# Rows of two expert tables fetched together: one 8 KB fetch a token and slot in a ring of two, in place of two 4 KB fetches in a ring of four

## The reference, cut to what matters

```
ub = u_tab[eb]
vb = v_tab[eb]
a = jax.nn.gelu(jnp.einsum('td,ted->te', xb, ub, preferred_element_type=jnp.float32))
return jnp.einsum('te,ted->td', (gb * a).astype(vb.dtype), vb)
```

## Time and profile before

| what | us |
|---|---|
| time, median of 3 runs | 2168.68 (2165.64 to 2168.92) |
| span of the profiled execution, first to last instruction | 2161.6 |
| median less that span | 7.1 |
| PE busy in the span | 2121.7 (98%) |
| DVE, ACT, POOL busy | 1442.4, 858.3, 1038.6 |

### The profile page before, as it was taken

How to read it: one execution, slowest core, us unless ns; L and a number is a source line. 1 busy time by engine, 2 the same in 40 slices (tenths; PEclk the granted TensorE clock), 3 DMA queues, 4 the chain that set the end, 5 groups by cost and what they waited for, 6 DMA issues and landing times.

```text
span 2161.6 us, 29125 instructions
## 1 busy us (share of the span) xinstructions
PE 2121.7 (98%) x10648; PEld 1837.8 (85%) x10648; DVE 1442.4 (67%) x2713; ACT 858.3 (40%) x1306; POOL 1038.6 (48%) x573
## 2 busy tenths in 40 slices
PE   8989999999999999999999999999999999999999
PEld 7857888888877877899999999999998888888887
DVE  5973411110054995369998777787867999999987
ACT  4354522232264454253334444444433333333332
POOL 1203244443423333435566888888863444444342
PEclk9999999999999999999999999999999999999999
DMA  4202344444442222334347899998899999999996
GB/s 177 82 27 62 104 117 127 117 119 115 117 118 74 86 71 77 117 106 121 112 147 207 242 267 321 284 315 249 261 309 318 388 388 371 373 375 377 369 359 251
DMA packets 240489, 444.14 MB, mean 205 GB/s; under 512 B 102459, under 2 KB 152028, under 8 KB 240220
## 3 DMA queue, kind: packets, MB, share of 16 engines
q1 hardware_dynamic: 152060, 299.07, 41.8%
q0 software_dynamic: 55488, 134.83, 19.3%
q10 hardware_dynamic: 32800, 8.39, 1.8%
HBM read 397.71 MB, written 44.50 MB: 205 GB/s over the span
## 4 chain that ended last, share of the span: by engine, by line
PE 69%; POOL 13%; DVE 8%; issue 4%; DMA 3%; ACT 2%; SPq 0%; DVEq 0%; ACTq 0%; POOLq 0%
PE bank L469 22%; PE bank L473 22%; PE bank L472 22%; POOL gate_matrices L1151 9%; POOL y L1160 4%; DMA y<-in_peer_u_rows,gidx 3%; DVE m L1979 1%; PE bank L923 1%; DVE xn L1980 1%; DVE WL L2297 1%; PE bank L645 1%; DMA wraw<-in_peer_u 1%; ACT sc L1302 1%; DVE y L2308 0%; DVE hots L2329 0%
## 5 line engine op out<-in xcount | busy, mean ns | idle before, releaser
L1140 POOL TENSOR_TENSOR WL<-wraw,WH 128x1024 fp32r<-128x1024 f32 x171 | 435.9, 2552 | 723.5 <-ACT WH L1191 723.5
L1191 ACT ACTIVATE WH<-wraw 128x1024 fp32r<-128x1024 f32 x411 | 435.0, 1060 | 627.4 <-PE bank L469 393.6
L469 PE MATMUL bank<-XH,WH 128*128 128x384 f32 (+2 forms) x1864 | 668.8, 359 | 12.6 <-DVE WL L2297 7.8
L473 PE MATMUL bank<-XH,WL 128*128 128x384 f32 (+2 forms) x1864 | 657.8, 353 | 0.0
L472 PE MATMUL bank<-XL,WH 128*128 128x384 f32 (+2 forms) x1864 | 657.6, 353 | 0.0
L469 PEld LDWEIGHTS bank<-XH,WH 128*128 128x128 f32 x1864 | 351.4, 189 | 46.3 <-issue 12.9
L472 PEld LDWEIGHTS bank<-XL,WH 128*128 128x128 f32 x1864 | 351.6, 189 | 29.0 <-issue 0.7
L473 PEld LDWEIGHTS bank<-XH,WL 128*128 128x128 f32 x1864 | 351.1, 188 | 28.7
L2297 DVE TENSOR_TENSOR WL<-wraw,WH 128x1024 fp32r<-128x1024 f32 x240 | 293.0, 1222 | 57.6 <-ACT WH L1191 51.8
L469 PE MATMUL bank<-WH,GH 128*128 128x512 f32 x768 | 298.9, 389 | 1.6 <-issue 1.6
L473 PE MATMUL bank<-WH,GL 128*128 128x512 f32 x768 | 298.8, 389 | 0.0
(11 more groups left out here) (313 smaller groups left out, 2561.8 us busy)
## 6 DMA issues: line engine op xcount, KB each, us to landing
wraw<-in_peer_u SPq DMA_DIRECT2D x128, 512.0 KB
wraw<-in_peer_v SPq DMA_DIRECT2D x128, 512.0 KB
activations<-ac SPq DMA_DIRECT2D x122, 192.0 KB
ar<-activations SPq DMA_DIRECT2D x122, 192.0 KB
gr<-gate_matrices SPq DMA_DIRECT2D x124, 128.0 KB
wraw<-in_w_gate SPq DMA_DIRECT2D x22, 512.0 KB
wraw<-in_w_up SPq DMA_DIRECT2D x22, 512.0 KB
wraw<-in_w_down SPq DMA_DIRECT2D x22, 512.0 KB
```

Of the source, the lines that this page charges most:

```text
L469: mm = pe.matmul(out, wh, xh, start=first, stop=False)
L473: return pe.matmul(out, wl, xh, start=False, stop=last)
L1140: pool.tensor_tensor(WL[:, u % NW, 0:m], wraw[:, u % NR, 0:m], WH[:, u % NW, 0:m].bitcast(F32), ALU.subtract).then_inc(s("w_lo"), 1)
L1191: act.activation(WH[:, u % NW, 0:k * n], wraw[:, u % NR, 0:k * n], ACT.Copy).then_inc(s("w_hi"), 1)
```

## The change

The two tables are laid side by side in memory, so that one indirect DMA of 8 KB a token brings the rows of u and v of one slot. There are 128 such fetches of 1 MB, in a ring of two buffers of 8 KB a partition. Each slot is finished before its buffer is free: DVE makes the dot product, ACT applies Gelu and multiplies by the gate (two instructions on 128x1), and DVE adds the row of v one unit later. Steps 0 and 1 of the up stage have no slot, 53 slots are begun in the other 93 steps, and 75 in the down stage. The scatters stand 1, 3, 3, 3, 3, 3 to the slots, so that 128 are out after 48 slots.

```diff
-NGATHER = 4
-EARLY = 2
-SCATTERS = [0, 2, 1, 2, 1, 2, 2, 1, 2, 1, 2]
+NGATHER = 2
+SLOTS_UP = 53
+SCATTERS = [1, 3, 3, 3, 3, 3]
-UP_ROWS_1, UP_ROWS_2 = 112, HS
+def slots_until(step):
+    if step < 2:
+        return 0
+    if step <= ups:
+        return (step - 1) * SLOTS_UP // (ups - 1)
+    return SLOTS_UP + min((step - ups) * (HS - SLOTS_UP) // (NEXP - 4), HS - SLOTS_UP)
+def slots_of(step):
+    return range(slots_until(step), slots_until(step + 1))
...
+        u_row, v_row = ([gathered[:, n, at:at + D] for n in range(NGATHER)] for at in (0, D))
+        uv_rows = A["peer_uv_rows"]
...
-            for row in range(2 * HS):
-                if row >= NGATHER:
-                    pool.wait_ge(s("rows_used"), row - NGATHER + 1)
+            for k in range(HS):
+                if k >= NGATHER:
+                    pool.wait_ge(s("rows_used"), k - NGATHER + 1)
+                pool.indirect_dma_start(out=gathered[:, k % NGATHER, :], out_offset=None, in_=uv_rows[:, :],
+                                        in_offset=bass.IndirectOffsetOnAxis(ap=gidx[:, k:k + 1], axis=0)
+                                        ).then_inc(s(f"row_landed{k % NGATHER}"), 16)
+                for n in range(scattered_until(k), scattered_until(k + 1)):
+                    scatter(n)
...
+            def activate_slots(step):
+                for k in slots_of(step):
+                    if k == 0:
+                        act.wait_ge(s("gates_copied"), 1)
+                    act.wait_ge(s("dots"), k + 1)
+                    act.activation(gdot[:, k:k + 1], gdot[:, k:k + 1], ACT.Gelu_apprx_tanh).then_inc(s("dots_active"), 1)
+                    act.wait_ge(s("dots_active"), k + 1)
+                    act.activation(gdot[:, k:k + 1], gdot[:, k:k + 1], ACT.Copy, scale=ggate[:, k:k + 1]).then_inc(
+                        s("slots_active"), 1)
...
+            def dot_slot(k):
+                dve.wait_ge(s(f"row_landed{k % NGATHER}"), 16 * (k // NGATHER + 1))
+                if k == 0:
+                    dve.wait_ge(s("x_nat_made"), 1)
+                at = u_row[k % NGATHER]
+                dve.tensor_tensor_reduce(out=at, in0=at, in1=x_nat[:, :], scale=1.0, scalar=0.0, op0=ALU.mult, op1=ALU.add,
+                                         accum_out=gdot[:, k:k + 1]).then_inc(s("dots"), 1)
+            def add_slot(k):
+                dve.wait_ge(s("slots_active"), k + 1)
+                if k:
+                    dve.wait_ge(s("rows_used"), k)
+                dve.scalar_tensor_tensor(out=hN[:, NTD, :], in0=v_row[k % NGATHER], scalar=gdot[:, k:k + 1],
                                          in1=hN[:, NTD, :], op0=ALU.mult, op1=ALU.add).then_inc(s("rows_used"), 1)
+            def use_slots(step):
+                for k in slots_of(step - 1):
+                    add_slot(k)
+                for k in slots_of(step):
+                    dot_slot(k)
...
-                for row in range(EARLY):
-                    use_row(row)
-                    use_rows(x - FIRST_GATE_UP)
+                    use_slots(x - FIRST_GATE_UP)
...
-    laid["peer_u_rows"] = laid["peer_u_2"][0]
+    laid["peer_uv_rows"] = _np.concatenate([laid["peer_u_2"][0], laid["peer_v_2"][0]], 1)
```

More of the change, by code:

```diff
@@ L94, in fours_of, with scattered_until @@
     return range(FIRST_FOUR + b * fours // GATE_UPS, FIRST_FOUR + (b + 1) * fours // GATE_UPS)
-def rows_until(slot):
+def slots_until(step):
     ups = NEXP - FIRST_GATE_UP
-    after = min(slot, GATE_UPS) + max(min(slot, ups) - GATE_UPS, 0)
-    rest = 2 * HS - EARLY - ups
-    return EARLY + after + min(max(slot - ups, 0) * rest // (NEXP - 4), rest)
-def scattered_until(row):
-    heads, part = divmod(row, len(SCATTERS))
+    if step < 2:
[5 more added lines that the diff above has]
+    return range(slots_until(step), slots_until(step + 1))
+def scattered_until(slot):
+    heads, part = divmod(slot, len(SCATTERS))
     return min(heads * SEL + sum(SCATTERS[:part]), HS)
-def slot_after_row(row):
-    return next(n for n in range(3 * NEXP) if rows_until(n) > row)
 def t5_bucket(dist):
@@ L1156, in _ @@
             pool.wait_ge(s("index_made"), 1)
-            for row in range(2 * HS):
-                if row >= NGATHER:
-                    pool.wait_ge(s("rows_used"), row - NGATHER + 1)
-                pool.indirect_dma_start(out=gathered[:, row % NGATHER, :], out_offset=None,
-                                        in_=(u_rows if row < HS else v_rows)[:, :],
-                                        in_offset=bass.IndirectOffsetOnAxis(ap=gidx[:, row % HS:row % HS + 1], axis=0)
-                                        ).then_inc(s(f"row_landed{row % NGATHER}"), 16)
-                for k in range(scattered_until(row), scattered_until(row + 1)):
-                    scatter(k)
-                if scattered_until(row) == HS > scattered_until(row - 1):
+            for k in range(HS):
[6 more added lines that the diff above has]
+                    scatter(n)
+                if scattered_until(k + 1) == HS > scattered_until(k):
                     pool.wait_ge(s("scattered"), 16 * HS)
@@ L1623, in copy_gates @@
                     act.dma_start(gd.rearrange("i j t -> j i t")[:, :, tt * GTOK:(tt + 1) * GTOK], Gs[:, tt % 2, :, :]).then_inc(s(f"g_out{tt}"), 16)
-            def activate_rows(slot):
-                for n, (first, end) in enumerate(((0, UP_ROWS_1), (UP_ROWS_1, UP_ROWS_2))):
-                    if slot == slot_after_row(end - 1) + 2:
-                        act.wait_ge(s("rows_used"), end)
-                        act.activation(gdot[:, first:end], gdot[:, first:end], ACT.Gelu_apprx_tanh).then_inc(
-                            s("rows_active"), 1)
+            def activate_slots(step):
[7 more added lines that the diff above has]
+                        s("slots_active"), 1)
             def high_weighed(x):
@@ L1643, in down @@
                         high_weighed(x + 2)
[L1644 removed]
+                    activate_slots(NEXP - FIRST_GATE_UP + x)
             prepare()
@@ L2319, in use_rows @@
-            def use_rows(slot):
-                for row in range(rows_until(slot), rows_until(slot + 1)):
-                    use_row(row)
+                at = u_row[k % NGATHER]
[6 more added lines that the diff above has]
+                dve.scalar_tensor_tensor(out=hN[:, NTD, :], in0=v_row[k % NGATHER], scalar=gdot[:, k:k + 1],
+                                         in1=hN[:, NTD, :], op0=ALU.mult, op1=ALU.add).then_inc(s("rows_used"), 1)
```

26 lines of the change are left out of this document (3 added, 23 removed).

## The result

The changed kernel takes 2209.17 us (median of 4 runs, 2202.44 to 2210.11) against 2168.80 us of the kernel before (4 runs beside it, 2165.64 to 2172.99): ratio 1.0168, 95% interval 1.0148 to 1.0188. The forecast was 2164.0 us, range 2159 to 2192. It was wrong in sign and outside its range. The first rival happened, the ring of two.

What follows compares the result with a forecast made beforehand. PE, busy in 98% of the span, was taken as the bound, with only 8.6 us of idle to save. Span 2161.6 - 4.7 = 2156.9 us, plus 7.1 us around it, gave 2164.0 us; range 2159 to 2192.

Steps and rivals of the forecast that it cites:

- The first rival: Down stage: the ring of two sets the pace if a fetch takes over 8.9 us; 2195 us at 9.9 us; chance 0.27.
- The floor: Whole span: at most PE's 8.6 us of idle can be saved, so the span can't fall below 2153.0 us.
- POOL in the up stage: POOL was full, 435 of 446 us, and set the rows' pace; after the change 362 us, at most 428.
- the list of signs: What would show the forecast right, such as up-stage row waits under 40 us and POOL's idle there ended by adds.
- The start of the up stage: Before 1215 us: with no slot in steps 0 and 1, PE's 4.7 us of waits go; bounds 0 and 8.6.
- ACT: Both stages: two small instructions and semaphores, some 0.7 us a slot, cost nothing; DVE waits for ACT in the up stage.
- The ring: Down stage: a fetch takes 7.7 us where 8.9 are allowed, leaving 1.2 us of room a cycle; cost 0.
- The lag: Down stage: a late row only moves DVE inside its unit; it may lag 5.8 us before PE stands, by `WL`.
- The rival's price: Down stage, ring of two: at a 9.9 us fetch (8.5 + 1.4) the cycle is 14.5 us, giving 2195 us.
- Around the span: Outside the span: 7.1 us, as in the median before, added to the span of 2156.9 us.

Runs made afterwards that it cites:

- before_late_start: The kernel before, with no fetched row used before step 2 of the up stage and 163 rows instead of 159 in the down stage; 2152.63 us, ratio 0.9918.
- low_first: The changed kernel with `low` put before the add and the dot of a unit in the down stage; 2200.69 us, ratio 1.0139.
- half_fetch: The changed kernel with each fetch bringing only u's 4 KB a token, the add reading the same buffer; 2171.82 us, ratio 0.9996.
- gl_ahead: The changed kernel with `low_weighed` two units ahead and before the dot in the down stage, the add before it; 2190.65 us, ratio 1.0097.
- split_fetch: The changed kernel with two 4 KB fetches a slot in the same two buffers, u refetched after its dot, v after its add; 2185.65 us, ratio 1.0078.
- add_after_weigh: The changed kernel with the add of the last unit's slot moved between `weigh` and `low_weighed` in the down stage; 2169.05 us, ratio 0.9986.

## Why the prediction was wrong, step by step

**The floor** held: nothing but PE's idle time could be saved, and `before_late_start` came down to it (span 2151.0 against the 2153.0 worked out; 2.5 us of it lie outside the two stages). It left one thing out: a wait can also cost clock, 1.7 us in the kernel before.

**POOL in the up stage: right in size, wrong as a cause.** The fetch took 1.33 us there, as assumed, and POOL's idle was ended by adds (87.9 us), as the list of signs said. But "it is full", "the rows arrive at POOL's pace" did not explain DVE's waits of the earlier trace rows. POOL made as many scatters and nearly as many fetches in `before_late_start` and waited for DVE; what was missing was its lead.

**The start of the up stage: right.** No wait of PE stands before 1215 us, DVE's waits for rows fell to 23.8 us (under 40 was the mark), and the stage is 5.5 us shorter against the 4.7 taken. Part of the agreement is luck: the eight profiled kernels with this up stage and 8 KB fetches took 462.1 to 469.2 us in it, against one trace of before. `before_late_start` shows that the later first use alone is enough for the gain; fewer fetches aren't needed.

**ACT: right in size.** Its two instructions take 0.20 and 0.295 us, and in the down stage ACT was in time. In the up stage DVE waited 23.8 us for it, as foretold. In the kernel as changed I see no wait of PE that comes from it; in `low_first` ACT's waits for dots are part of what holds up `WH`.

**The ring: here it failed.** "At 7.7 us the ring has 1.2 us of room a cycle." The allowance, 13.5 us less 4.6, was right: dot to release measured 3.30 + 1.28 = 4.58 us. The fetch was not: 10.6 us instead of 7.7 where DVE waited for it, so a turn of 15.4 us where 13.5 were allowed. Two terms of that were mis-sized. POOL's own part was taken as unchanged at 1.31 us. It was 2.43 in the mean (1.45 in the down stage of before) and 3.0 in the fetches that DVE waited for: 1.7 of the 2.9 us. The second is the flight behind it, 7.6 us in these fetches against 7.7 - 1.31 = 6.4: the 6.27 us of the earlier trace rows came from the up stage, and its single row is not this stage's. The sum also left out the 0.28 us from the release to the fetch. I had the earlier trace rows with 2.68 us on POOL and 10.55 us to the dot, and set it aside because "these had other fetches of the same queue before them". "With starts 6.75 us apart there is rarely one" was wrong too: a fetch that takes over 6.75 us is never alone, and the prediction's own 7.7 us is over it. The two in the timeline run from 1980.99 to 1991.95 and from 1987.62 to 1998.63. The added 4 KB, the term that the change was about, was right: 1.3 us (`half_fetch`) against the 1.4 added.

The Trainium skill, page "DMA: Bandwidth & Descriptors", section "Anatomy of one DMA — SWDGE (gpsimd) path", gives by its fit an estimate of 2.0 + 2.4 = 4.4 us for such a fetch. The measurement differs (7.6 us behind the issue, with the DMA engines 93% busy), and decides.

**The lag: wrong in its place.** "DVE may lag 5.8 us before PE stands" went by `WL`, wanted two units after. `low_weighed` makes `GL` for the next unit and stands directly in front of the wait for the row, so a late row delays the next unit's `GL`, and PE stands after one unit's room. By the sum it matters little: with a turn 1.34 us too long any lag is used up after a few turns. No run shows that by itself, since `gl_ahead`, which has more lag, brought other waits in.

**The rival's price.** It was given 2195 us at a fetch of 9.9 us, against 2209 measured. Its 8.5 us before the added 1.4 came from no row. At 10.6 us in every turn it would have been 2195 + 37.5 x 0.7 = 2221; 22 of the 68 fetches were not waited for, so the mean turn was 14.84 us and not the 15.2 of that sum. The room of "a slower PE leaves the DMAs more room" was small (DMA share 0.93 against 0.97), and the fetch was not quick for it.

**Around the span: wrong.** 7.1 us was taken from a median and the span of one execution; it is 2.1 us. The profiled execution of before was a quick one (about 2163.7), and the forecast stood 5 us too high against its own sum. This decides nothing here.

**Open.** How much a short issue alone would give back, since `low_first` brought another wait in; why the issue is held up, and why not each time; how much of `split_fetch` is the earlier release; 5 us of the down stage; the 7 us of `before_late_start` that no span shows.

## What to carry to other kernels

Before a ring is made shorter, add up one whole turn (use, release, issue, flight, landing to next use) from rows of the busy stage where it will run, take the longest fetch seen there rather than a quiet one, and compare with the turn that the bounding engine allows: here 13.5 us were allowed and the mean turn was 14.8, which cost 52 us; a third buffer took back all but 3. Joining two fetches also joins their releases: the first half's buffer is given back only with the second's. And where a producer is hardly faster than its consumer, a consumer that starts too early may wait for it through the whole stage; try a later first use before cutting the producer's work.

## What the runs showed of the hardware

**A POOL fetch is longer to issue beside some of DVE's work.** In the changed kernel's down stage its instruction took 0.94 us while DVE was idle. Where it began beside `low` it took 2.68 us, if DVE went on through the two `ga` and `GL` and stopped, and mostly 3.82 with a dot and a further `low` behind them. In `low_first` it took 1.08 us beside the two `ga` and `GL`, though DVE was busy then too. It can be seen in before as well: 2.68 us. So how busy DVE is does not decide alone. What runs beside it doesn't either: in `add_after_weigh` the same sequence of DVE gave 1.01 us 28 times and over 3 us eight times. The Trainium skill, page "SBUF — State Buffer", section "Who interferes with whom", has DVE and GpSimd share one pair of SBUF ports under an exclusive lock, and has a DVE instruction with two SBUF inputs contend with a GpSimd instruction that reads SBUF. The longer issues agree with that (all of these DVE instructions have two inputs there); the short ones beside the same instructions it does not explain. The same section says that `tensor_tensor` did not stall a DMA of GpSimd in a probe, and infers the reason; the 2.68 and 3.82 us here against 0.94 speak against that for this indirect DMA. No run here took the two inputs away, so the cause is not shown.

**Short waits can cost PE more than their length.** Behind four of its waits in the down stage, the shortest of 1.82 us, the matmuls ran for 3.4 us at the lower clock level. The length of the wait does not tell alone: behind one of 3.36 us and one of 2.58 us the clock stayed up.

**A threshold.** With three or four buffers two slots take 13.4 to 13.5 us, which is PE's own pace, and the stage 526 to 529 us; the ring then has room for 20 or 27 us a turn. With two buffers, the turns of 13.66, 13.98 and 14.84 us went with 533.1, 540.3 and 574.7 us. The slope, some 36 us for each us of turn ((574.7 - 526) / 1.34), is near the 37.5 turns of the stage by count alone, and `low_first` (14.56 us, 564.1) lies on it whatever its waits are. So the slope proves no cause. What shows the ring is that the stage returns to PE's pace once it has a third buffer.
